# A two-layer encoder on one core: the first two tiles of each layer's first product moved ahead of the layer loop and to its end

## The reference, cut to what matters

```python
h = layer_norm(x, ln_in_g, ln_in_b)                    # x: 512 tokens x 1024
for l in range(2):
    proj = h @ w_in[l]                                  # 1024 x 2048
    a_q, a_k, a_v, b_u, b_b, b_c, c_u, d_q, d_k, d_v = split_columns(proj)
    ...                                                 # four head groups: attention, conv, Fourier, attention
    h = layer_norm(DN_ALPHA * h + mix @ w_out[l], ln1_g[l], ln1_b[l])
    ffn = jnp.square(jax.nn.relu(h @ w1[l])) @ w2[l]    # 1024 x 4096 and back
    h = layer_norm(DN_ALPHA * h + ffn, ln2_g[l], ln2_b[l])
return h
```

## Time and profile before

| What | Value |
| --- | --- |
| median of 3 runs | 1070.69 us (1069.56 to 1070.83) |
| the profiled execution | 1069.36 us, with a span of 1067.3 us |
| TensorE, products | busy 1052.7 us, 99% of the span |
| DVE, ACT, POOL | busy 73%, 49%, 9% |
| granted TensorE clock, mean | 0.998 |
| chain of work that ended last | TensorE 97%, POOL 1% |

### The profile page before, as it was taken

One profiled execution on the slowest core, in us unless ns is written; L12 is line 12 of the kernel. 1 busy time (PEld: TensorE's weight loads), 2 busy tenths in 40 slices (PEclk: granted clock), 3 DMA queues, 4 the chain that ended last, 5 costly groups with the idle time before them and its releaser, 6 DMA issues.

```text
span 1067.3 us, 15600 instructions
## 1 busy us (share of the span) xinstructions
PE 1052.7 (99%) x5310; PEld 895.5 (84%) x5310; DVE 782.7 (73%) x1087; ACT 525.2 (49%) x789; POOL 98.7 (9%) x90
## 2 busy tenths in 40 slices
PE   7999999999999999999999999999999999999996
PEld 6888889998888888888888888899888888888885
DVE  8845886968758758758887568777794784785786
ACT  3433666365355355355634247653643643652653
POOL 5200232100000000000002003221000000000003
PEclk9999999999999999999999999999999999999999
DMA  7432023031521520431343410310234134125122
GB/s 289 158 119 79 1 61 120 2 126 38 200 79 40 181 95 32 169 115 40 119 144 137 158 40 21 119 41 16 112 120 157 40 112 164 39 88 187 39 79 80
DMA packets 17382, 105.54 MB, mean 99 GB/s; under 512 B 2016, under 2 KB 2704, under 8 KB 5792
## 3 DMA queue, kind: packets, MB, share of 16 engines
q1 hardware_dynamic: 15984, 98.70, 25.7%
q0 software_dynamic: 1184, 5.86, 1.7%
q10 hardware_dynamic: 144, 0.07, 0.0%
HBM read 101.49 MB, written 2.10 MB: 97 GB/s over the span
## 4 chain that ended last, share of the span: by engine, by line
PE 97%; POOL 1%; ACT 0%; issue 0%; DVE 0%; DVEq 0%; POOLq 0%; ACTq 0%
PE bank L455 19%; PE bank L456 18%; PE bank L457 18%; PE bank L762 9%; PE bank L764 9%; PE bank L763 9%; PE bank L705 4%; PE bank L691 2%; PE bank L464 1%; PE bank L602 1%; PE bank L603 1%; PE bank L536 1%; PE bank L615 1%; PE bank L527 1%; PE bank L528 1%; POOL x L1818 1%
## 5 line engine op out<-in xcount | busy, mean ns | idle before, releaser
L455 PE MATMUL bank<-h_hi,w_hi 128*128 128x512 f32 (+1 forms) x704 | 260.6, 370 | 0.0
L456 PE MATMUL bank<-h_lo,w_hi 128*128 128x512 f32 (+1 forms) x704 | 260.3, 370 | 0.0
L457 PE MATMUL bank<-h_hi,w_lo 128*128 128x512 f32 (+1 forms) x704 | 260.3, 370 | 0.0
L762 PE MATMUL bank<-w_hi,hid_hi 128*128 128x512 f32 x448 | 174.4, 389 | 0.0
L763 PE MATMUL bank<-w_lo,hid_hi 128*128 128x512 f32 x448 | 174.3, 389 | 0.0
L764 PE MATMUL bank<-w_hi,hid_lo 128*128 128x512 f32 x448 | 174.3, 389 | 0.0
L1193 DVE TENSOR_TENSOR w_lo<-w_raw,w_hi 128x2048 fp32r<-128x2048 f32 x62 | 141.9, 2288 | 36.8 <-ACT w_hi L879 30.0
L457 PEld LDWEIGHTS bank<-h_hi,w_lo 128*128 128x128 f32 x704 | 132.6, 188 | 22.5
L455 PEld LDWEIGHTS bank<-h_hi,w_hi 128*128 128x128 f32 x704 | 132.7, 188 | 22.4
L456 PEld LDWEIGHTS bank<-h_lo,w_hi 128*128 128x128 f32 x704 | 132.7, 188 | 22.4
L879 ACT CAST w_hi<-w_raw 128x2048 fp32r<-128x2048 f32 x56 | 107.1, 1913 | 78.8 <-PE bank L764 56.4
(11 more groups left out here) (180 smaller groups left out, 1647.3 us busy)
## 6 DMA issues: line engine op xcount, KB each, us to landing
w_raw<-in_weights SPq DMA_DIRECT2D x63, 1024.0 KB, 4.8
w_third<-in_weights SPq DMA_DIRECT2D x23, 1024.0 KB, 4.8
rows<-in_rows POOLq DMA_DIRECT2D x4, 1024.0 KB, 5.1
w_raw<-in_weights SPq DMA_DIRECT2D x4, 512.0 KB, 7.5
out_h<-x SPq DMA_DIRECT2D x8, 256.0 KB, 2.0
x<-in_x SPq DMA_DIRECT2D x3, 512.0 KB, 9.5
dft<-in_dft SPq DMA_DIRECT2D x2, 512.0 KB, 7.1
qk_gain<-in_qk_gain POOLq DMA_DIRECT2D x3, 192.0 KB, 3.4
```

The costliest lines, as they stand in the source:

```text
L455: pe.matmul(dst, s_hi, m_hi, start=first, stop=False)
L456: pe.matmul(dst, s_hi, m_lo, start=False, stop=False)
L457: return pe.matmul(dst, s_lo, m_hi, start=False, stop=last)
L762: pe.matmul(bank[dst + t][:], s_hi, m_hi, start=start, stop=False, skip_group_check=goes_on)
```

## The change

TensorE: the 8 transposes of `keep_warm` ahead of the first turn become 1, and the 6 behind it go. Layer 0's work on tiles 0 and 1 stands ahead of the loop in an order of its own; that of layer 1 stands at the end of the loop body, under a condition on `l`, in the order that it had. DVE: between tile 0's norm and tile 1's, the subtraction of tile 0's first half now stands between the two statistics of tile 1, and tile 2's gain is read from the banks. POOL: `rstd(3)` stands ahead of the last tile-2 additions. The two outputs of tile 3 are issued by ACT instead of SP.

```diff
@@ SP @@
-            for t in range(TOK):
+            for t in range(TOK - 1):
                 for half in range(2):
-                    if t < TOK - 1:
-                        sp.wait_ge(last_normed, 2 * t + half + 1)
-                    else:
-                        sp.wait_ge(sems["normed"], (2 * DEPTH) * (2 * TOK) + half + 1)
+                    sp.wait_ge(last_normed, 2 * t + half + 1)
@@ TensorE @@
-            keep_warm(8)
-            turn(0, 0)
-            keep_warm(6)
-            with pe.Fori(0, DEPTH) as l:
...
+            def own_high(l, t, kts):
+                for kt in kts:
+                    if kt % 4 == 0:
+                        wait(pe, l, "h_hi", 2 * t + kt // 4 + 1)
+                    if t == 0:
+                        high_part_ready(l, kt // PARTS, kt % PARTS)
+                    dst, t_hi, _, m_hi, _ = first_group(t, kt)
+                    pe.matmul(dst, t_hi, m_hi, start=kt == 0, stop=False)
+
+            def own_low(l, t, kts):
+                for kt in kts:
+                    if kt % 4 == 0:
+                        wait(pe, l, "h_lo", 2 * t + kt // 4 + 1)
+                    dst, _, t_lo, m_hi, _ = first_group(t, kt)
+                    pe.matmul(dst, t_lo, m_hi, start=False, stop=False)
+
+            def weights_low(l, t, kts):
+                for kt in kts:
+                    if t == 0:
+                        part_ready(l, kt // PARTS, kt % PARTS)
+                    dst, t_hi, _, _, m_lo = first_group(t, kt)
+                    done = pe.matmul(dst, t_hi, m_lo, start=False, stop=kt == KT - 1)
+                    if kt == KT - 1:
+                        done.then_inc(sems["products"], 1)
+
+            def first_tiles(l):
                 for t in range(2):
                     for kt in range(KT):
                         if t == 0 and kt == 4:
                             turn(l, 1)
...
+                        own_high(l, t, (kt,))
+                        own_low(l, t, (kt,))
+                weights_low(l, 0, range(KT))
+                turn(l, 2)
+                weights_low(l, 1, range(KT))
+
+            keep_warm(1)
+            turn(0, 0)
+
+            own_high(0, 0, range(2))
+            own_low(0, 0, range(2))
+            weights_low(0, 0, range(2))
+            for kt in range(2, KT):
+                own_high(0, 0, (kt,))
+                own_low(0, 0, (kt,))
+            turn(0, 1)
+            weights_low(0, 0, range(2, 4))
+            own_high(0, 1, range(KT))
+            own_low(0, 1, range(KT))
+            weights_low(0, 0, range(4, 6))
+            weights_low(0, 1, range(4))
+            turn(0, 2)
+            weights_low(0, 0, range(6, KT))
+            weights_low(0, 1, range(4, KT))
+            with pe.Fori(0, DEPTH) as l:
...
                 chunk(CHUNKS - 1, True)
+                with pe.If(l < DEPTH - 1):
+                    first_tiles(l + 1)
@@ ACT, its last instructions @@
+            for half in range(2):
+                act.wait_ge(sems["normed"], (2 * DEPTH) * (2 * TOK) + half + 1)
+                c = slice(half * BANK, (half + 1) * BANK)
+                act.dma_start(out[TOK - 1, :, c], x[:, TOK - 1, c]).then_inc(out_written, 16)
@@ DVE @@
-                    if which or t < 2:
+                    if which or t < TOK - 1:
...
-            input_stats(1)
-            stream_low(0, 0, 0)
+            dve.wait_ge(x_landed[1], 16)
+            row_stats(1, 0)
+            low_half(0, 0, 0, 0)
+            row_stats(1, 1)
+            variance(1, 4, 2, LN_EPS)
+            low_half(0, 0, 0, 1)
             first_norm(1)
@@ POOL @@
             layer_norm_rstd(2 * DEPTH, 2, 3)
+            layer_norm_rstd(2 * DEPTH, 3)
             add_offset(2, 0)
-            layer_norm_rstd(2 * DEPTH, 3)
             add_offset(2, 1)
```

More of the change, by code:

```diff
@@ L507, in _, with first_group @@
                     last.then_inc(first_spread, 1)
-            keep_warm(8)
-            turn(0, 0)
-            keep_warm(6)
-            with pe.Fori(0, DEPTH) as l:
-                def first_group(t, kt):
-                    c = slice(t * P, (t + 1) * P)
-                    return (bank[t][:], h_hi[:, kt, c], h_lo[:, kt, c], *w_cols(kt // 4, kt % 4, BANK, 0, BANK))
+            def first_group(t, kt):
+                c = slice(t * P, (t + 1) * P)
+                return (bank[t][:], h_hi[:, kt, c], h_lo[:, kt, c], *w_cols(kt // 4, kt % 4, BANK, 0, BANK))
+            def own_high(l, t, kts):
[21 more added lines that the diff above has]
+            def first_tiles(l):
                 for t in range(2):
```

## The result

The changed kernel takes 1074.96 us (median of 7, 1073.59 to 1075.80) against 1070.39 us (median of 7, 1069.56 to 1070.83): slower, ratio 1.0044 with a 95% interval of 1.0035 to 1.0053. The forecast was 1068.4 in a range up to 1070.5. The profiled execution took 1075.80 us with a span of 1073.8, 6.5 more than before.

A forecast was written before the change was run, and what follows sets the result against it. TensorE, busy 99% of the span, was taken as the bound, so time is won only in opening and tail: -1.95 + 0.15 - 0.5 = -2.3 us from 1070.69, giving 1068.4, range 1066.9 to 1070.5.

The forecast's parts named there:

- the loop's turn: TensorE's layer loop now turns ahead of tile 2's products: a cost of +0.15 us, ends 0 and 1.7.
- Rival A: At tile 2 of layer 1 TensorE waits as ACT did: +1.7 instead of +0.15, 1069.9 us; chance 0.12.
- rival C: Opening: without 14 transposes the clock rises later, 18 products and 16 transposes run slow: +2.4 us, 1073.1; chance 0.07.
- the lower level that I read there: Opening: TensorE's clock at 1.2 GHz, rising to 2.4 as the first 16 transposes with loads ended.
- The opening: Up to tile 2's first product: first product 1.71 us earlier, 0.24 less idle and restarts; 1.95 saved, 24.88 to 22.9.
- The tail: Last tile's end: earlier rstd(3) and scaling, last issue 0.4 us earlier, less crowded transfers; 0.5 saved, ends 0 and 0.9.
- rival B: The tail gives nothing if POOL's addition and the shared transfers set the end: -1.8 us, 1068.9; chance 0.12.
- the waits for DVE at 540 would swallow what is saved at 535: Layer 1's start: the same tiles wait for DVE at 540.22, so removing the old turn's gap at 535 gains nothing.

The follow-up runs named there:

- e4: Changed kernel with TensorE's two layers written out by a plain Python loop instead of the Fori: 1068.09 us, ratio 0.9980.
- e6: Changed kernel with layer 1's weight blocks 2 and 3 loaded later and four unread transposes ahead of TensorE's loop: 1068.57 us, ratio 0.9986.
- e9: Changed kernel with layer 1's tiles 0 and 1 under a condition at the loop's start, and four unread transposes ahead of the loop: 1068.49 us, ratio 0.9987.
- e10: Kernel before the change with TensorE's two layers written out instead of looped: 1070.35 us, ratio 1.0002.
- e3: Changed kernel with one SP wait made later, so layer 1's distance table and weight blocks 2 and 3 load after tiles 0 and 1: 1073.09 us, ratio 1.0028.
- e8: Kernel before the change with four added 512 KB copies issued by SP while TensorE's loop turns: 1075.55 us, ratio 1.0041.
- e1: Kernel before the change with only TensorE's layer loop turned at the new place, all 14 transposes kept: 1072.16 us, ratio 1.0027.
- e5: Changed kernel with four unread transposes directly ahead of TensorE's loop, moving its start by 8 instructions: 1069.60 us, ratio 1.0000.
- e7: Kernel before the change with TensorE's loop turned at the new place and keep_warm cut from 14 transposes to 1: 1075.93 us, ratio 1.0061.
- e2: Changed kernel with layer 1's tiles 0 and 1 put back at the loop's start under a condition: 1071.23 us, ratio 1.0010.

## Why the prediction was wrong, step by step

The step that failed is the loop's turn, which I took at +0.15 with 1.7 as its upper end. In the profiled execution it was +8.0. The rest of the sum came close: without the long stalls, e4, e6 and e9 are 2.0, 1.6 and 1.6 us below the kernel before that ran beside them, where 2.3 was forecast (e6 and e9 pay 0.44 for their four transposes). That their 1068.1 to 1068.6 fall on the 1068.4 of the forecast is in part luck, since I had subtracted from a median of three executions, 1070.69, which later stood at 1070.07 to 1070.39.

- I read 0.11 us between two products as the price of the branch. It was only what stuck out: the branch took 3.47 us in the same trace, under 3.6 us of queued work. The view of the `Fori`'s line had it, and I had not asked for it. Rival A named the right place and part of the mechanism, at too small a price. I priced it by ACT's gap of 1.70, which is another engine's, and again only what stuck out: in the view of ACT's loop line the branch stands at 536.2 and the next instruction at 538.8, 2.6 us later, and ACT was at work until 537.2. I then argued that 2.7 us of queued work would cover it; the cover was 3.0, and the branch alone needs 3.4 when nothing is in its way. So even with quiet DMA engines and no second fetch in the way the turn costs 0.5 us: from tile 2's first product to the last product of the kernel it is 1033.6 us in e6 and e9, and 1033.1 before, in e4 and in e10.
- I left out what the DMA engines do at the new place. Blocks 2 and 3 of the weights are loaded there, and e3 and e8 show that this makes the branch long: 3.4 to 3.8 without traffic, 4.5 to 7.7 with it. Why the fetch's packet comes so late no run tells: it came behind the ebb of the traffic in the changed kernel, in e1, e5 and e7, but in the midst of it, 5.3 us after the branch, in e8.
- The fetch of the second block was not in the prediction at all. The Trainium skill, Runtime: NRT & Kernel Launch, section Instruction fetch mechanics, which I had cited for the first fetch, also says that an engine's instructions come in blocks of 256 (16 KiB). The trace agrees in size: 40 packets of q8 with 0.66 MB, 16.5 KB each. Dropping 13 transposes put the loop's start close to the end of a block; e5, e7 and e9 show what that costs, a stop of 2 to 3 us, and in e3 and e7 the clock with it.
- The clock was rival C's subject, at the wrong place. In the opening the view of windows has the granted clock at 1.00 from the start, before and after, so the lower level that I read there stands on the distance of the loads alone: 0.21 apart until 7.6 before, and already about 0.1 at 8.15 in the changed kernel. The moment differs between executions, and not with the transposes: in e1, with all 14, loads are still 0.21 apart at 8.5, and in e2 the first product is slow too (and six transposes of tile 0's turn take 1.49 us against 1.00 in e9). So C's loss of 14 slow products is in no trace, but part of the opening's spread is of this kind. Where the 8.0 us were lost, the clock fell in the first stop, and 2.0 of them are its price.
- The opening: forecast 1.95, found 1.35 in this profile. Its start depends on when tile 1 and the weights land: here DVE waited for tile 1 until 9.29 instead of 8.65. Over the profiles, tile 2 starts on average at 25.24 in the five with the old opening (24.88 to 25.62) and at 23.43 in the four with the new one and no transposes added (22.82 to 24.02): 1.8 us. In e3, where tile 1's statistics start at 8.85, it is 22.82, close to the 22.9 worked out; in e2, where they start at 8.95, it is 23.36. The step holds within this spread. One term of its sum was misread: between the halves of tile 1's turn 1.31 - 0.27 + 0.11 is 1.15, so 0.3 lay idle and not 0.2.
- The tail: forecast 0.5, found 0.18 in each profile with the change. All steps came as written (`rstd(3)` early, DVE's last scaling 0.42 earlier, the last issue at 5.93 behind the last product instead of 6.43), but the span ends 9.18 behind it instead of 9.36. The last four transfers of 256 KB share the DMA engines without a pause, so the time of the last issue was probably not what set the end; no run parts the two. That is rival B's reason.
- That the waits for DVE at 540 would swallow what is saved at 535 holds where the branch is gone: e10 has no gap at 535 and still takes 1033.1 us from tile 2's first product to the last one, as before.

## What to carry to other kernels

A loop's branch back is a transfer: ask how long the branch itself took, how much work is queued over it, what else the DMA engines carry at that moment, and how many instructions lie between the loop's start and the end of its block, since the next one comes only some 3 us after the first. An edit far ahead of a loop moves its start; when a change costs microseconds at a place that it didn't touch, look for stalls with no releaser, and where the view names one, compare its end with that of the branch. If the program can be written out, as in e4 and e10, the question goes away.

## What the runs showed of the hardware that was not expected

- TensorE's taken branch back over the layer loop (over the body of a layer, half of the page's 5310 products and transposes) took 3.4 to 3.8 us with quiet DMA engines (before, e2, e3, e6, e9) and 4.5 to 7.7 us with traffic (after, e1, e5, e7, e8). The short loop over the inner chunks, taken in the same kernels, took 0.24 us.
- With quiet engines the fetch's packet came 1.0 to 1.1 us after the branch began and took 0.9 to 1.4 us, and the sequencer went on about 1.4 us behind its end. The packet of the next block came 3.0 to 3.6 us after the first (4.7 in e8), in all kernels that loop, whether TensorE stopped for it (after, e2, e3, e7) or not.
- The granted clock fell to 0.5 within single stops of 3.9 us (after, at 550.7) and 4.2 (e8, at 537.9), within the second of two stops of 1.6 and 2.0 (e7, at 552.9), and behind two of 0.5 and 2.6 (e3), when TensorE had been at work again for 1 us; in the profiled executions it did not fall with single stops of 2.5 (e2) and 1.9 (e5). In five of e2's eleven executions the mean clock is 0.995 or 0.996 where the profiled one has 0.997, so it may have fallen there.
